# Where the modulation's accumulation steps stand in a two-block transformer kernel: beside the feed-forward chunks only, with sums in two buffers and native one-column products

## The reference, cut to what matters

```python
c_act = jax.nn.silu(c)
for l in range(DEPTH):
    mod = c_act @ w_ada[l] + b_ada[l]          # [1, 1024] @ [1024, 6144]
    sh1, sc1, g1, sh2, sc2, g2 = jnp.split(mod, 6, axis=-1)
    h = modulate(rmsnorm(x, norm_mix_g[l]), sh1, sc1)
```

## Time and profile before

| | before |
|---|---|
| median of 3 runs | 2279.82 us (2277.78 to 2280.36) |
| the profiled execution's own time | 2277.41 us |
| its span in the trace | 2275.5 us |
| PE / weight loads / DVE / ACT busy, share of the span | 95% / 84% / 78% / 61% |
| mean granted TensorE clock | 0.966 |
| first-block mixers | about 23 to 172 us and 381 to 530 us |
| feed-forward parts | 172 to 376, 530 to 735, 887 to 1075 us |
| last stage, the experts | from 1240 us to the end |

### The profile page before, as it was taken

How to read it: one execution, slowest core, us unless ns; L and a number is a source line. 1 busy time by engine, 2 the same in 40 slices (tenths; PEclk the granted TensorE clock), 3 DMA queues, 4 the chain that set the end, 5 groups by cost and what they waited for, 6 DMA issues and landing times.

```text
span 2275.5 us, 31145 instructions
## 1 busy us (share of the span) xinstructions
PE 2169.1 (95%) x12670; PEld 1901.7 (84%) x12670; DVE 1783.1 (78%) x2276; ACT 1394.4 (61%) x1974; POOL 2.2 (0%) x17
## 2 busy tenths in 40 slices
PE   6989998999998998999997999999999999999998
PEld 6779998878998788999887888887888787887876
DVE  6568877757887856766766889888888989888987
ACT  4345544345554655444755777677777777777875
POOL 0000000000000000000000000000000000000000
PEclk9789999889999999999998999999999999999999
DMA  6336765424666413766512899899989999999985
GB/s 246 107 136 232 244 228 199 176 105 179 243 227 236 161 72 130 259 222 231 186 57 111 322 361 357 335 347 347 369 339 346 346 354 352 343 348 344 367 345 192
DMA packets 89428, 574.87 MB, mean 253 GB/s; under 512 B 10048, under 2 KB 10048, under 8 KB 31040
## 3 DMA queue, kind: packets, MB, share of 16 engines
q1 hardware_dynamic: 87984, 566.89, 66.9%
q0 software_dynamic: 288, 3.15, 0.4%
q10 hardware_dynamic: 1008, 2.79, 0.3%
HBM read 571.75 MB, written 1.05 MB: 252 GB/s over the span
## 4 chain that ended last, share of the span: by engine, by line
PE 82%; DVE 11%; ACT 4%; issue 2%; DMA 1%; SPq 0%; DVEq 0%; ACTq 0%
PE bank L2033 40%; PE bank L479 40%; DVE wlo L1389 3%; ACT whi L984 1%; DVE arena L1786 1%; DMA side<-in_w_ada 1%; PE bank L2091 1%; DVE RSTD L1455 1%; DVE extra_lo L1389 1%; DVE side L1488 1%; DVE XC L1422 0%; ACT extra_hi L984 0%; DVE XC L1464 0%; DVE RSTD L1414 0%; DVE XC L1444 0%
## 5 line engine op out<-in xcount | busy, mean ns | idle before, releaser
L1389 DVE TENSOR_TENSOR wlo<-ring,whi 128x1024 fp32r<-128x1024 f32 (+1 forms) x766 | 877.2, 1176 | 149.4 <-ACT whi L984 139.2
L984 ACT ACTIVATE whi<-ring 128x1024 fp32r<-128x1024 f32 (+1 forms) x766 | 757.7, 1019 | 195.5 <-PE bank L479 115.4
L479 PE MATMUL bank<-HH,whi 128*128 128x256 f32 x1536 | 445.1, 290 | 10.2 <-DVE HL L1507 6.3
L479 PE MATMUL bank<-HH,wlo 128*128 128x256 f32 x1536 | 437.6, 285 | 0.0
L479 PE MATMUL bank<-HL,whi 128*128 128x256 f32 x1536 | 437.0, 284 | 0.0
L479 PEld LDWEIGHTS bank<-HH,whi 128*128 128x128 f32 x1536 | 295.9, 193 | 19.1 <-issue 8.9
L479 PEld LDWEIGHTS bank<-HL,whi 128*128 128x128 f32 x1536 | 296.5, 193 | 0.4
L479 PEld LDWEIGHTS bank<-HH,wlo 128*128 128x128 f32 x1536 | 296.4, 193 | 0.0
L1389 DVE TENSOR_TENSOR extra_lo<-ring,extra_hi 128x1024 fp32r<-128x1024 f32 x224 | 264.2, 1219 | 14.8 <-ACT extra_hi L984 14.4
L984 ACT ACTIVATE extra_hi<-ring 128x1024 fp32r<-128x1024 f32 x224 | 229.8, 1061 | 52.9 <-PE bank L2033 52.9
L2033 PE MATMUL bank<-whi,xg 128*128 128x512 f32 x672 | 222.3, 399 | 0.0
(11 more groups left out here) (293 smaller groups left out, 3621.6 us busy)
## 6 DMA issues: line engine op xcount, KB each, us to landing
ring<-in_moe_gate SPq DMA_DIRECT2D x112, 1024.0 KB, 5.3
ring<-in_moe_up SPq DMA_DIRECT2D x112, 1024.0 KB, 6.5
ring<-in_moe_down SPq DMA_DIRECT2D x112, 1024.0 KB, 5.3
side<-in_w_ada SPq DMA_DIRECT2D x96, 512.0 KB, 4.4
ring<-in_w_up SPq DMA_DIRECT2D x44, 1024.0 KB, 4.9
ring<-in_w_in SPq DMA_DIRECT2D x32, 1024.0 KB, 5.7
ring<-in_w_down SPq DMA_DIRECT2D x32, 704.0 KB, 4.2
ring<-in_ffn_gu SPq DMA_DIRECT2D x22, 1024.0 KB, 4.8
```

The costliest lines, as they stand in the source:

```text
L479: return pe.matmul(out, lhsT, rhs, start=start, stop=stop, skip_group_check=True)
L984: a.activation(hi, part, ACT.Copy).then_inc(*made.up(("hi", n, i)))
L1389: v.tensor_tensor(lo, part, hi.bitcast(F32), ALU.subtract).then_inc(*done.up(("lo", n, i)))
```

## The change

All 96 sum steps now stand beside feed-forward chunks, one per call without pauses between groups (36 calls in each of the three parts). All calls in the first-block mixers are gone, on PE, ACT, DVE and SP. The sum alternates between two buffers (`side_acc`, the second in the place of `acc_hi`), the fp32r halves and ACT's part are gone, and PE adds over the partitions by 8 native fp32 matmuls of one column against `ones`. The bias is added beside slice 2 of the next group. `cact` is made in the first up chunk's iteration. The first two slices are loaded behind the last `w_out` chunk of layer 0.

```diff
@@ pe_program @@
             def modulation():
-                yield
+                for _ in range(9):
+                    yield
                 for l in range(DEPTH):
                     for g in range(6):
-                        for _ in range(10):
+                        b = take("mod", l, g, until=[(v_mod, "mod", l, g)])
+                        pe.wait_ge(*v_mod("acc", 8 * (6 * l + g) + 7))
+                        for j in range(8):
+                            tm = mm(b[:, j:j + 1], side_acc[g % 2][:, 128 * j:128 * j + 128], ones[:, 0:1], True, True)
+                        tm.then_inc(*p_mod.up(("mod", l, g)))
+                        for _ in range(8):
                             yield
-                        b = take("mod", l, g, until=[(v_mod, "mod", l, g)])
-                        pe.wait_ge(*v_mod("lo", l, g))
-                        for j in range(8):
-                            js = slice(128 * j, 128 * j + 128)
-                            mm(b[:, 2 * j:2 * j + 2], acc_hi[:, js], one_r[:, :], True, False)
-                            tm = mm(b[:, 2 * j:2 * j + 2], acc_lo[:, js], one_r[:, :], False, True)
-                        tm.then_inc(*p_mod.up(("mod", l, g)))
-                        yield
                 while True:
                     yield
@@ act_program: in the mixers, and in the up and down loops @@
-            def modulation():
...
-                        a.wait_ge(*v_mod("acc", 8 * (6 * l + g) + 7))
-                        a.activation(acc_hi[:, :], side_acc, ACT.Copy).then_inc(*a_mod.up(("hi", l, g)))
...
-                    next(mod)
+                    elif l == 0:
+                        a.wait_ge(s_vec, 16)
+                        a.activation(cact[:, :], W("c", 0, 8), ACT.Silu).then_inc(*a_mod.up(("cact",)))
@@ dve_program @@
             def modulation():
+                def add(l, g):
+                    v.wait_ge(*p_mod("mod", l, g))
...
                 yield
...
+                for n in range(96):
+                    k, at = n % 8, side_acc[n // 8 % 2]
+                    v.wait_ge(s_side[n % 2], 16 * (n // 2 + 1))
+                    if k == 0:
+                        v.wait_ge(*a_mod("cact"))
+                        if n >= 16:
+                            v.wait_ge(*p_mod("mod", *divmod(n // 8 - 2, 6)))
+                        v.tensor_scalar(at, side_in[n % 2], cact[:, 0:1], None, ALU.mult).then_inc(*v_mod.up(("acc", n)))
+                    else:
+                        v.wait_ge(*v_mod("acc", n - 1))
+                        v.scalar_tensor_tensor(at, side_in[n % 2], cact[:, k:k + 1], at, ALU.mult, ALU.add).then_inc(
+                            *v_mod.up(("acc", n)))
+                    if k == 2 and n > 8:
+                        add(*divmod(n // 8 - 1, 6))
+                    yield
+                for _ in range(4):
+                    yield
+                add(DEPTH - 1, 5)
@@ dve_program, pe_program and act_program: 13 calls per mixer on each @@
-                for _ in range(2):
-                    next(mod)
...
@@ pool_program @@
-            g.tensor_copy(one_r[:, :], ones[:, 0:2]).then_inc(*g_mod.up(("one",)))
@@ sp_program @@
-                    if n % 8 == 1:
-                        for _ in range(3 if n > 8 else 1):
-                            yield
...
                 if key[0] in ("w_up", "ffn_gu"):
-                    return key[-1] > 1
+                    return key[-1] > 1 and (key[0] != "w_up" or key[-2:] != (0, 2))
                 if key[0] in ("w_down", "ffn_down"):
                     return 1
-                if key[0] == "w_in":
-                    return (0, 0, 2, 2, 2, 1)[key[2]] if key[2] else 2
-                return 2 if key[0] in ("w_v", "w_xp") else 0
+                return 0
...
-                if n == NSLOT - 1:
+                if n == CH["w_out", 0, 3]:
                     next(mod)
```

90 lines of the change are left out of this document (5 added, 85 removed).

## The result

| | before | after |
|---|---|---|
| median | 2278.0 us (2275.6 to 2280.4, 6 runs) | 2287.6 us (2282.5 to 2296.2, 6 runs) |
| ratio, 95% interval | | 1.0043 [1.0023, 1.0063] |
| the profiled execution: own time, span | 2277.4, 2275.5 us | 2286.8, 2285.0 us |
| mean granted clock | 0.966 | 0.960 |

The changed kernel is slower by 0.4%, some 10 us. The forecast was 2286.4 us. The two traces say how far its parts came out as well.

What follows compares the result with a forecast made beforehand. PE's stream of matmuls and its gaps were taken as the bound. Terms -15.1 + 4.6 + 1.0 + 12.7 + 3.4 = +6.6 us on a median of 2279.8 gave 2286.4 us, range 2271 to 2296 (the forecast's own 2280 to 2294).

Steps and rivals of the forecast that it cites:

- Mixers, -15.1: Both first-block mixers: removing the modulation steps saves 15.1 us of PE's waits, products and lower clock; lower bound 8.6 us.
- The rival that the clock isn't given back: Mixers: removing the steps saves 8.6 instead of 15.1 us, giving 2292.9 us; chance 0.11.
- Products, +4.6: Feed-forward parts: twelve groups of eight native products at 1.8 us, less ten at 1.7 before, add 4.6 us (3.0 to 5.4).
- the rival of 2308 us: Native products take twice their row's passes, as with four passes: 21.6 us on top of the sum; chance 0.03.
- Up chunks, +1.0: First block's up chunks: PE's product waits 0.2 us for the sum in each of five groups, 1.0 us (0 to 3).
- Down chunks, 16.0 us of waits: Beside down chunks: PE waits four times for the sum, 4.5, 3.7, 3.8 and 4.0 us; 12.7 us more than before (8 to 20).
- The clock, +3.4: Behind the down-chunk waits: three stretches at lower clock, less one before, lose 3.4 us more (0 to 10).
- the floor case: Beside down chunks: four waits of 3.0 us at their floor and no lower clock, total -1.8, 2278.0 us; chance 0.25.
- The late slices: Feed-forward parts: a load takes 7 us under denser traffic, costing about 10 us, giving 2297 us; chance 0.08.
- The hidden wait: Beside down chunks: DVE reaches its sum before PE ends the chunk, so total -10.5, 2269.3 us; chance 0.12.

Runs made afterwards that it cites:

- e9: Kernel before with only the products changed: eight native one-column products straight from the sum, no `acc_hi` or `acc_lo`, steps unmoved; 2260.3 us, ratio 0.9914.
- e1: Changed kernel with PE's product step one call later, two calls behind the eighth sum instead of one; 2259.3 us, ratio 0.9903.
- e3: Changed kernel with the same step numbers, but PE's call beside down chunks placed behind the chunk's 33 matmuls instead of ahead; 2263.7 us, ratio 0.9928.
- e8: e1 with each group's eight one-column products done twice; 2301.1 us, ratio 1.0101.
- e10: e5 with eight extra one-column products of constants right behind each group's eight; 2287.1 us, ratio 1.0035.
- e11: e5 with eight extra one-column products of constants per group, placed four calls later; 2270.0 us, ratio 0.9959.
- e13: Changed kernel with all steps of DVE, PE and SP one call later, sum and product still one call apart; 2297.0 us, ratio 1.0071.
- e6: Changed kernel with only the first two slices of `w_ada` loaded, 94 transfers and their waits left out; 2286.3 us, ratio 1.0042.
- e5: Changed kernel with PE's product step two calls later, three calls behind the eighth sum; 2248.9 us, ratio 0.9879.
- e4: Changed kernel with DVE's sum beside a down chunk ahead of the subtraction for the chunk after next, not behind it; 2285.6 us, ratio 1.0026.
- e7: e4 with only the first two slices of `w_ada` loaded; 2267.1 us, ratio 0.9955.

## Why the prediction was right

The forecast was right in sign, in size and in the mechanism that decided it, the waits for the sum. That it came within 1.2 us is luck: the clock cost some 10 us more than forecast, and a term that the prediction doesn't have, closer matmuls in the down chunks, gave 8 us back. Point by point:

- **Mixers, -15.1.** Measured -14.4. The stretches are as named, 3.28 and 14.21 us. But in layer 0 one more thing happens than the prediction had: the clock, at 1.00 for the native products (the 0.84 of the earlier trace rows is gone), now falls earlier in the score products, for 20.5 us from 82.7 on instead of 17.1 from 92.6 on. And what the prediction ascribed to the steps' leaving is by e9's profile mostly the work of the shorter group: no `acc_lo`, no rounding on ACT ahead of the split. Moving the steps away added 2.2 and 1.9 us in these profiles, which one profile each can't tell from nothing. The rival that the clock isn't given back (8.6 us saved) is not borne out by 12.2 to 14.4 us, but nothing here shows how much of the gain is clock.
- **Products, +4.6.** A group takes 1.70 us at full clock (1.78 beside the first up chunk), the forecast 1.8; two more groups in the feed-forward parts are 3.4 us. The trace has 16 records for eight products and 1.70 us, and doubling them added 1.79 us a group, so the rival of 2308 us is out. By the rule of the Trainium skill (FP8 and Floating Point Precision, TensorE Precision Notes: true fp32 takes four passes) the prediction estimated a group at 3.6 us. That reading of the rule fails for one-column products; the rule itself is not refuted, since a record need not be one pass. In the kernel before, the 16 native products of 256 columns in the second block's first up chunk leave 32 records, 0.216 us apart at full clock: 0.43 us a product, 3.6 times the 0.119 us of an fp32r product of that width, which is close to four.
- **Up chunks, +1.0.** By the idle times of PEld it is 0.31, 0.31, 0.24 and 0.30 us for four of the five groups and nothing for the fifth, 1.2 us. Right.
- **Down chunks, 16.0 us of waits.** Measured 18.1 us, in exactly the four places. The lower bound of 3.4 us for the first chunk of a tile was read rightly from the earlier trace rows, but it holds for DVE as early as it is there. These rows of DVE's timeline stand between those of the earlier trace rows:

```profile
1047.01 1.28 DVE L1488 SCALAR_TENSOR_TENSOR side<-side,cact 128x1024 f32<-128x1024 f32 x1
1048.21 0.48 DVE L1764 SCALAR_TENSOR_TENSOR xT<-bank,modT,xT 128x256 f32<-128x256 f32 x1
```

  The previous sum ends at 1048.29, 1.1 us before PE's end of the chunk (1049.43). In the changed kernel it ends at most 0.9 us before and up to 0.6 us after that end; why DVE is later there was not tried (the first and the last wait stand at the second tile of their part, the second and the third in the first block, where the norm is longer). For the last wait this alone makes 3.4 + 1.2 = 4.6 us, which is what was measured (4.64). The third is 3.4 + 0.2 and the first block's extra norm instruction, the second the same with 0.5 us more of lag and the slice (0.47). The estimates 4.5, 3.7, 3.8 and 4.0 became 4.29, 5.12, 4.04 and 4.64 us: 2.1 us short in all, most of it in the second wait, where neither the slice nor the longer norm was counted.
- **The clock, +3.4.** The large miss. The four waits have not one 3.4 us stretch behind three of them, but together 28 us of work at 0.50, with the products inside; the two stretches beside up chunks match the two of before. That is some 14 us of loss, not 3.4. The prediction read the price of one wait of 2 us and multiplied it; behind waits of 4 to 5 us the stretches are 6.8 and 10.2 us long, not 3.4. Its upper bound, 10, was too low as well.
- **What made up for it.** 14.8 us of added waits (18.1 less 3.3), 1.2, 3.4 and some 14 make +33 us in the feed-forward parts, but these grew by 24.7 us. The missing 8 us are PE's: its matmuls in the down chunks start closer to each other than before. Three windows of 8 us inside down chunks at full clock, from the kernel before, e9 and the changed kernel (columns as above; the count behind PE's busy time is what matters):

```profile
1054.00:1062.00 8.00, 8.00 (x70) 8.00 (x69) 6.60 (x9) 3.47 (x6) 0.00 (x0) 1.00 0.90 315
```

```profile
1040.00:1048.00 8.00, 8.00 (x70) 8.00 (x69) 5.99 (x8) 3.25 (x5) 0.00 (x0) 1.00 0.83 309
```

```profile
1066.00:1074.00 8.00, 8.00 (x73) 8.00 (x72) 4.98 (x8) 3.48 (x5) 0.00 (x0) 1.00 0.59 191
```

  From start to start it is 0.119 us in the kernel before (both profiles) and in e9, and 0.114 us in the changed kernel and in every relative of it (e1, e3 to e8, e10, e11, e13). There are 3 x 16 x 33 = 1584 such matmuls, so 5 ns each make 8 us. It is not the traffic: e6, without the loads, has 0.114 as well. The matmuls of the up chunks, which read `HH` and `HL`, stay at 0.119 us in all of them. The change also takes away the buffer `one_r`, which is allocated ahead of `arena`, where these matmuls' operands `midh` and `midl` lie, and behind `HH` and `HL`; e9 keeps it. That the place of the operands matters is a guess that fits these facts; no run tests it, and the cause stays open. The prediction had no term for it, and put what the change does to `one_r` at nothing.

  e5 is the same work without waits: its feed-forward parts take 626.3 us, those after 660.9, those before 636.2. So the changed kernel's waits and their clock cost 34.6 us. The kernel before, with two groups (3.4 us) fewer, stands 9.9 us above e5; of these 13.3 us the matmul spacing makes 8, its waits 3.7, which leaves 1.6 for its two stretches at 0.50.

Of the rivals, the floor case (four waits of 3 us and no lower clock) is refuted by the rows. The late slices are refuted by e6 as a cost of 10 us: without the loads the time is the same, and two of the waits are 0.5 us shorter. The hidden wait, the only rival that would have made the change faster, describes e5: with the product two calls later it is true, and worth 38.7 us.

The changed kernel is thus two edits of opposite sign. The native products, alone, give 18.7 us (e9). The denser placement takes that and 10 us more, because the product was put one call behind the sum: with three calls it is 11.4 us better than e9 instead of 27.3 us worse. But 8 of these 11.4 us are the closer matmuls, and e5's profile has the short first mixer, so that placing all sums beside feed-forward chunks pays by itself is not shown.

## What to carry to other kernels

Where one engine uses at a fixed place what another makes, count the distance between the two in the first engine's work. Include in the maker's time what it can begin only when the user has finished (here a rounding and a subtraction) and what stands ahead of it on its own engine at that moment (here an earlier sum, a residual, a norm): 4 to 5 us against a distance of zero. In this kernel, waits of 4 to 5 us on TensorE cost up to twice their length, since the clock fell with them; and a move is tested best with the distance as a parameter of one number. If doubling an operation costs twice what its rows say, look at the clock behind it before believing in a higher price. Compare also, before and after, the start-to-start time of matmuls that the change isn't meant to touch: here 8 us lay in it.

## What the runs showed of the hardware

- **The clock also fell behind one-column products without idle time.** In e10 3.49 us of them in a row are followed by 3.4 us or more at 0.50 in ten of twelve places; in e11 1.71 us of them in none of 24. The same instructions in one piece or in two differ by 17 us in the total (e10, e11).
- **The clock of a stage with the same instructions differs from run to run.** The stages ahead of FF 1 have the same instructions on PE, DVE and ACT in the changed kernel, e1, e3 to e8, e10 and e11, yet mixer 0 took 142.0, 144.7, 142.5, 143.0, 131.0, 135.0, 142.0, 144.6, 135.0 and 142.7 us. The mean clock of that stage was 0.96 in the fastest, e5, and 0.84 in the slowest, e1 (windows, in that order):

```profile
23.60:154.70 131.10, 121.80 (x782) 107.30 (x782) 82.18 (x153) 63.51 (x123) 0.33 (x5) 0.96 0.34 123
```

```profile
23.60:168.30 144.70, 137.50 (x782) 117.58 (x783) 82.14 (x153) 63.66 (x123) 0.33 (x5) 0.84 0.31 112
```

DVE's and ACT's busy times are equal to 0.2 us; 16 us of PE's modelled busy time are not. The Trainium skill (TensorE: Matmul & The Clock Gate, What's actually happening) says that one kernel can show different numbers of slow matmuls from run to run; the traces agree: apart from the first and last few microseconds of this stage the clock is at 0.50 for 6.8 us in e5 and for 41 us in e1. Here it is worth up to 14 us in one stage, 0.6% of the whole, and no comparison of single profiles should be believed below that in this stage. Why the mixer falls to the lower clock at all was not tried.
- **Dependences travel over the issuing queue.** In e4 transfers of 4.2 us (median) made DVE wait 24.4 us in 19 places; in the place shown, the issue stood behind another transfer's wait. Without the loads (e7) the waits fell to about 1 us.
- **Matmuls of one shape can start 0.114 or 0.119 us apart at the same granted clock.** Every kernel without `one_r` has the first in its down chunks, the two with it (before, e9) the second; the cause is open.
